# The second feed-forward product of a two-layer encoder, by seven products of halves instead of eight

## The reference

```python
D_MODEL = 1024
SEQ = 512
DEPTH = 2
D_FF = 4 * D_MODEL
...
        h = layer_norm(DN_ALPHA * h + mix @ w_out[l], ln1_g[l], ln1_b[l])
        ffn = jnp.square(jax.nn.relu(h @ w1[l])) @ w2[l]
        h = layer_norm(DN_ALPHA * h + ffn, ln2_g[l], ln2_b[l])
```

## Time and profile before

| what | value |
|---|---|
| median of 3 runs | 1117.92 us (1117.54 to 1117.95) |
| the profiled execution, its own time | 1117.77 us |
| its span in the profile | 1116.1 us |
| TensorE busy | 1098.9 us (98%) |
| VectorE busy | 606.4 us (54%) |
| ScalarE busy | 391.5 us (35%) |
| GpSimd busy | 92.0 us (8%) |
| mean granted TensorE clock | 0.999 |

### The profile page before, as it was taken

How to read it: one execution, slowest core, us unless ns; L and a number is a source line. 1 busy time by engine, 2 the same in 40 slices (tenths; PEclk the granted TensorE clock), 3 DMA queues, 4 the chain that set the end, 5 groups by cost and what they waited for, 6 DMA issues and landing times.

```text
span 1116.1 us, 15149 instructions
## 1 busy us (share of the span) xinstructions
PE 1098.9 (98%) x5502; PEld 931.2 (83%) x5502; DVE 606.4 (54%) x908; ACT 391.5 (35%) x634; POOL 92.0 (8%) x84
## 2 busy tenths in 40 slices
PE   7999999999999999999999999999999999999997
PEld 6888889988888888888878888889888888888886
DVE  7846887853443334336657478787532542433446
ACT  3433665351232232142124256553411511421410
POOL 5200222100000000000102013221000000000001
PEclk9999999999999999999999999999999999999999
DMA  7432032142223113114203410313322223123202
GB/s 276 151 114 76 1 95 77 41 156 77 98 76 128 75 75 150 75 76 151 76 7 147 151 38 21 113 39 122 113 110 79 78 96 127 75 75 139 79 10 75
DMA packets 16800, 104.38 MB, mean 94 GB/s; under 512 B 1952, under 2 KB 2384, under 8 KB 5216
## 3 DMA queue, kind: packets, MB, share of 16 engines
q1 hardware_dynamic: 15408, 97.59, 23.6%
q0 software_dynamic: 1184, 5.86, 1.6%
q10 hardware_dynamic: 144, 0.07, 0.0%
HBM read 100.37 MB, written 2.10 MB: 92 GB/s over the span
## 4 chain that ended last, share of the span: by engine, by line
PE 94%; DVE 4%; issue 1%; DMA 1%; ACT 0%; DVEq 0%; SPq 0%
PE bank L366 28%; PE bank L367 28%; PE bank L368 28%; PE bank L616 3%; PE bank L602 2%; PE bank L513 1%; PE bank L514 1%; PE bank L375 1%; DMA x<-in_x 1%; DVE x L1033 1%; PE bank L526 1%; PE bank L447 1%; DVE mx L1257 0%; DVE h_lo L1054 0%; DVE bn L1015 0%
## 5 line engine op out<-in xcount | busy, mean ns | idle before, releaser
L366 PE MATMUL bank<-h_hi,w_hi 128*128 128x512 f32 (+1 forms) x704 | 260.8, 370 | 0.1
L367 PE MATMUL bank<-h_lo,w_hi 128*128 128x512 f32 (+1 forms) x704 | 260.3, 370 | 0.0
L368 PE MATMUL bank<-h_hi,w_lo 128*128 128x512 f32 (+1 forms) x704 | 260.3, 370 | 0.0
L366 PE MATMUL bank<-w_hi,hid_hi 128*128 128x512 f32 x512 | 199.3, 389 | 0.0
L367 PE MATMUL bank<-w_lo,hid_hi 128*128 128x512 f32 x512 | 199.2, 389 | 0.0
L368 PE MATMUL bank<-w_hi,hid_lo 128*128 128x512 f32 x512 | 199.2, 389 | 0.0
L756 ACT CAST w_hi<-w_raw 128x2048 fp32r<-128x2048 f32 x60 | 112.3, 1908 | 245.1 <-PE bank L368 220.3
L366 PEld LDWEIGHTS bank<-h_hi,w_hi 128*128 128x128 f32 x704 | 132.7, 188 | 23.4 <-issue 0.9
L1367 DVE TENSOR_TENSOR x<-bank,x 128x512 f32<-128x512 f32 x64 | 44.2, 690 | 198.2 <-PE bank L368 197.9
L368 PEld LDWEIGHTS bank<-h_hi,w_lo 128*128 128x128 f32 x704 | 132.7, 188 | 22.5
L367 PEld LDWEIGHTS bank<-h_lo,w_hi 128*128 128x128 f32 x704 | 132.7, 188 | 22.2
(11 more groups left out here) (152 smaller groups left out, 1312.0 us busy)
## 6 DMA issues: line engine op xcount, KB each, us to landing
w_raw<-in_weights SPq DMA_DIRECT2D x86, 1024.0 KB, 4.8
rows<-in_rows POOLq DMA_DIRECT2D x4, 1024.0 KB, 4.9
w_raw<-in_weights SPq DMA_DIRECT2D x4, 512.0 KB, 7.5
out_h<-x SPq DMA_DIRECT2D x8, 256.0 KB, 2.0
x<-in_x SPq DMA_DIRECT2D x3, 512.0 KB, 9.6
qk_gain<-in_qk_gain POOLq DMA_DIRECT2D x3, 192.0 KB, 3.3
x<-in_x SPq DMA_DIRECT2D x2, 256.0 KB, 3.5
dft<-in_dft SPq DMA_DIRECT2D x1, 512.0 KB, 10.2
```

The source lines that it names most:

```text
L366: pe.matmul(dst, s_hi, m_hi, start=first, stop=False)
L367: pe.matmul(dst, s_hi, m_lo, start=False, stop=False)
L368: return pe.matmul(dst, s_lo, m_hi, start=False, stop=last)
```

## The change

The second stage of each chunk is computed from four quarters of the hidden matrix (A, tokens by hidden channels) and four of the weights (B, hidden channels by output channels). Halves of tokens are 256, halves of hidden channels 512 (the even and the odd tiles of the chunk), halves of output channels 512. With S1 = A21 + A22, S2 = S1 - A11, S3 = A11 - A21, S4 = A12 - S2 and T1 = B12 - B11, T2 = B22 - T1, T3 = B22 - B12, T4 = B21 - T2 the seven products are, in this order, A11 B11, S1 T1, S2 T2, S4 B22, S3 T3, A12 B21, A22 T4. Each has 2 tiles of 128 tokens, 4 steps and `three`: 24 matmuls of 128x512. A11 B11, S2 T2, S3 T3 and A22 T4 go on in the same two banks (6 and 7), S1 T1 and S4 B22 in banks 4 and 5, A12 B21 in its own two (2 and 3). After each product VectorE adds the banks as they stand to the stream: 14 additions a chunk.

What goes with it:

- ScalarE writes the relu to `y`, squares it there, and copies high parts of 256, 512 and 1024 columns; VectorE no longer squares. It makes the four sums (`hid_sum`, 256 columns each) for each of the 4 pairs of hidden tiles, and low parts of 256, 512 and 1024 columns.
- Eleven operands instead of eight blocks go through the split of each chunk. The four differences T1 to T4 are VectorE subtractions of 128x2048, written over a raw place.
- There is a third raw place, `w_third`, for B22, B21 and the next chunk's first block. To make room, working buffers of the attention part lie over the hidden ones, and `rope`, `dft`, `head_dft` and `dist` are loaded again for the second layer.
- The SP queue is written out. At the layer change it loads those four tensors and then the next weight blocks.
- GpSimd waits for the last hidden low part of the layer before it loads the normalisation rows, which lie in the same memory as `hid_sum`.
- The first four hidden tiles of chunks 2 to 4 no longer share their steps; all eight go one after the other.
- In the last chunk tiles 0 and 1 of the stream are finished by A12 B21, tiles 2 and 3 by A22 T4.

The core of the diff, constants first:

```diff
-CHUNK_G = 16
+HALF_TOK = SEQ // 2
+HALF_KT = KT // 2
+CHUNK_G = 22
+CHUNK_OPERANDS = 11
+W0, W1, W2, W3, B11, T1, T2, B22, T3, B21, T4 = range(CHUNK_OPERANDS)
+SLOT = (0, 1, 2, 3, 0, 1, 2, 3, 0, 1, 2)
+RELEASED = {W2: 0, W3: 0, B11: 2, T1: 4, T2: 6, B22: 8, T3: 10, B21: 12, T4: 14}
+NEXT_RELEASED = (18, 20)
...
```

The SP queue, per layer:

```diff
+                with sp.If(l > 0):
+                    wait(sp, l, "w_lo", 1)
+                    sp.dma_start(rope[:], rope_in).then_inc(const_landed, 16)
+                    sp.dma_start(dft[:], dft_in).then_inc(const_landed, 16)
+                    sp.dma_start(head_dft[:], head_dft_in).then_inc(const_landed, 16)
+                    sp.wait_ge(sems["products"], l * PER_LAYER["products"])
+                    sp.dma_start(dist[:], dist_in).then_inc(const_landed, 16)
...
+                    split_up_to(W0)
+                    if c == 0:
+                        load(b + 2, 0)
+                    else:
+                        load_third(b + 6)
+                    split_up_to(W1)
+                    load(b + 3, 1)
+                    split_up_to(W2)
+                    load(b + 4, 0)
+                    split_up_to(W3)
+                    load(b + 5, 1)
...
+                    split_up_to(B22)
+                    load_third(b + 7)
...
```

TensorE:

```diff
+                def half_product(a, b, dst, t, kt, first):
+                    q = slice(t * P, (t + 1) * P)
+                    s_hi, s_lo = hid_hi[:, kt, a, q], hid_lo[:, kt, a, q]
+                    m_hi, m_lo = w_cols(SLOT[b], kt, BANK, 0, BANK)
+                    start, stop, goes_on = first and kt == 0, kt == HALF_KT - 1, not first
+                    pe.matmul(bank[dst + t][:], s_hi, m_hi, start=start, stop=False, skip_group_check=goes_on)
+                    pe.matmul(bank[dst + t][:], s_hi, m_lo, start=False, stop=False, skip_group_check=goes_on)
+                    done = pe.matmul(bank[dst + t][:], s_lo, m_hi, start=False, stop=stop, skip_group_check=goes_on)
...
+                    for a, b, dst, first, n in ((S2, T2, 6, False, 1), (S4, B22, 4, False, 3), (S3, T3, 6, False, 5),
+                                                (A12, B21, 2, True, None), (A22, T4, 6, False, 9)):
+                        operand_ready(c, b)
+                        for t in range(2):
+                            if n is not None:
+                                added(n + t)
+                            for kt in range(HALF_KT):
+                                if last_chunk and b == T4 and (t, kt) == (0, 3):
+                                    with pe.If(l < DEPTH - 1):
+                                        turn(l + 1, 0)
+                                half_product(a, b, dst, t, kt, first)
...
```

VectorE in the second stage and at the end of a layer:

```diff
+                    other_quarters(3)
+                    add(0)
+                    low(T2)
+                    sum_weights(l, c, T3)
+                    add(1)
+                    low(B22)
+                    add(2)
+                    add(3)
+                    low(T3)
+                    add(4)
+                    add(5)
+                    sum_weights(l, c, T4)
+                    low(B21)
+                    add(6)
+                    add(7)
+                    low(T4)
+                    add(8)
+                    add(9)
+                    if not last:
+                        low(CHUNK_OPERANDS + W0)
+                        add(10)
+                        add(11)
+                        low(CHUNK_OPERANDS + W1)
+                        add(12)
+                        add(13)
+                        return
+                    k = 2 * l + 2
+                    add(10)
+                    variance(k, 0, 5)
+                    normalise(k, 0)
+                    add(11)
+                    variance(k, 1, 6)
+                    centre(k, 1)
+                    with dve.If(l < DEPTH - 1):
+                        stream_low(l + 1, 0, 0)
+                    scale(k, 1)
+                    with dve.If(l < DEPTH - 1):
+                        for part in range(PARTS):
+                            split_part(l + 1, 0, part)
+                        stream_low(l + 1, 0, 1)
+                    add(12)
+                    variance(k, 2, 7)
+                    normalise(k, 2)
+                    with dve.If(l < DEPTH - 1):
+                        for part in range(PARTS):
+                            split_part(l + 1, 1, part)
+                    add(13)
+                    variance(k, 3, 8)
+                    with dve.If(l < DEPTH - 1):
+                        stream_low(l + 1, 0, 2)
+                    normalise(k, 3)
```

More of the change, by code:

```diff
@@ L314, in turned_quad, with operand, raw_of @@
             return src, (slice(None), slice(2 * g, 2 * g + 2), slice(t * P, (t + 1) * P))
-        def chunk_bank(g, last):
-            return bank[(g + 4) % 8 if last else g]
+        def operand(l, c, i):
+            return l * PER_LAYER["w_lo"] + c * CHUNK_OPERANDS + (MLP0 + i)
+        def raw_of(i):
+            if i in (B22, B21, CHUNK_OPERANDS + W0):
+                return w_third[:]
+            return w_raw[:, 1 if i in (W1, W3, T3, CHUNK_OPERANDS + W1) else 0, :]
         block = ctx.enter_context(nc.Block())
@@ L646, in _, with hidden @@
                 side(last_sides[3])
[L649 to L650 removed]
+                def hidden(m, kt, t0, t1, first, last):
+                    s_hi, s_lo = w_cols(m // 2, kt, 2 * P, (m % 2) * P, P)
                     c = slice(t0 * P, t1 * P)
                     return three(bank[m][:, c], s_hi, s_lo, h_hi[:, kt, c], h_lo[:, kt, c], first, last)
[L654 to L669, removed]
[L670 to L678 removed]
@@ new lines, in add @@
+                    def add(n):
+                        p, t = n // 2, n % 2
+                        ready, dst, half, tile, before = ((1, 6, 0, 0, None), (3, 4, 1, 2, None), (5, 6, 1, 0, None), (7, 4, 1, 0, 4),
+                                                          (9, 6, 1, 2, 2), (11, 2, 0, 0, 0), (13, 6, 0, 2, None))[p]
+                        dve.wait_ge(sems["products"], l * PER_LAYER["products"] + c * CHUNK_G + (MLP_G0 + 8 + ready + t))
+                        dve.wait_ge(sems["added"], l * PER_LAYER["added"] + c * CHUNK_ADDS + (32 if before is None else 32 + before + t + 1))
+                        xs = x[:, tile + t, half * BANK:(half + 1) * BANK]
+                        dve.tensor_tensor(xs, bank[dst + t][:], xs, ALU.add).then_inc(sems["added"], 1)
+                        if last and p in (3, 4, 5, 6):
+                            wait(dve, l, "added", 32 + CHUNK_ADDS * (CHUNKS - 1) + n + 1)
+                            row_stats(tile + t, half)
@@ L1484, in _ @@
                 load_params(l + 1)
+                wait(pool, l, "hidden_lo", 12 * CHUNKS)
                 load_rows(2 * l + 2)
```

366 lines of the change are left out of this document (227 added, 139 removed).

## The result

| | before | after |
|---|---|---|
| median of 4 runs, us | 1117.93 (1117.54 to 1118.04) | 1082.52 (1081.60 to 1083.23) |
| ratio, 95% interval | | 0.9683 (0.9672 to 0.9695) |
| profiled execution, its span, us | 1117.77, 1116.1 | 1081.96, 1080.2 |

One further execution of the changed kernel (1329.5 us) and one of the kernel before (1379.9 us) ran at a mean granted clock of 0.75 and are left out; all other times are from executions at 0.98 or more.

What follows compares the result with a forecast made beforehand. TensorE, busy for 98% of the span, was taken as the bound. Chunks -43.5, end +5.3 and layer change +1.8 sum to -36.4 us from 1117.77, so 1081.4 by that clock, stated as 1081.5 us; range 1078.5 to 1091.

Steps and rivals of the forecast that it cites:

- eight chunks: Second stage: 168 matmuls for 192 saves 5.44 us in each of 8 chunks, -43.5 us; a chunk takes 81.6 us.
- the end: Behind the last matmul: VectorE finishes four tiles at E+9.9 in place of 4.6 us, +5.3 us.
- layer change: Between layers: VectorE's tiles, `h_lo` pairs and quarter splits delay tile 2's product, +1.8 us.
- no gain at all: Rival: matmuls going on in a bank already read cost 0.65 us more at 56 starts; about 1118 us, 2%.
- The added work: Per chunk beside TensorE: VectorE 60.0 us of 81.6, ScalarE 39 us, all hidden if operands are ready in time.
- The spares: Second stage of a chunk: no product waits for operands; smallest spare 2.5 us, so added work costs nothing.
- Late operands: Rival: spares of 2.5 to 4.5 us in the chunks are used up; 1084 to 1092 us, 14%.
- the walk: Step-by-step timing of a second stage from the last hidden tile's end T; chunk ends T+38.1, smallest spare 2.5 us.
- Four tiles at 4.51 from there: At the end: VectorE starts at tile 0's product, 8.16 us before TensorE's end E, and ends at E+9.9.
- The clock at the layer change: Rival: TensorE's pauses there drop the clock to 1.2 GHz, 16 matmuls cost 3.6 us more; 1085 us, 2%.
- VectorE as the bound: Rival: two-input VectorE work in the chunks is stretched past 81.6 us; at 1.5, 1149 us; 4%.
- point of break-even: Whole change lost when a chunk costs 4.5 us more than 81.6, at a VectorE stretch of 1.44.

Runs made afterwards that it cites:

- experiment 3: Changed kernel with B22's low part made twice in each chunk, 2.2 us more VectorE work; 1087.30 us.
- experiment 10: Changed kernel with B21's load issued when T3's low part is made, 3.6 us later, in every chunk; 1089.30 us.
- experiment 4: Changed kernel with B22's low part made three times in each chunk; 1113.3 us.
- experiment 1: Changed kernel with the difference T3 made ahead of the last hidden tile in every chunk; 1082.34 us, ratio 0.9682.
- experiment 2: Changed kernel without three of four contraction steps of S3 T3, 18 matmuls fewer per chunk, result incomplete; 1058.58 us.
- experiment 6: Changed kernel with A12 B21 ahead of S3 T3 in each layer's last chunk, so tiles 0 and 1 finish earlier; 1084.89 us.
- experiment 7: Changed kernel with A12 B21 ahead of S3 T3 in last chunks and the difference T3 made ahead of the last hidden tile; 1080.64 us.
- experiment 5: The changed kernel run again unedited; 1081.89, 1082.08, 1082.16, 1082.53 and 1083.30 us, the profiled run being the one of 1083.30.

## Why the prediction was right, point by point

The span fell by 35.9 us. The terms, as forecast and as measured in the profiles:

| term | forecast | measured | from |
|---|---|---|---|
| eight chunks | -43.5 | -43.5 | from tile 2's start to the last matmul 512.03 us for 533.80, twice |
| the end | +5.3 | +5.7 | 10.3 us for 4.6 behind the last matmul |
| layer change | +1.8 | +1.4 | 15.34 us for 13.94 |
| start of the program | 0 | +0.5 | first product at 12.22 us for 11.69 |
| sum | -36.4 | -35.9 | |

- **The matmuls.** Right. The seven products cost what 168 matmuls cost. Banks that are taken up again after a read cost nothing: no idle time before 448 matmuls of L750, and chunks of 81.6 us. The rival "no gain at all" is out. It had counted 56 such starts; there are 8 in a chunk, 64 in all, so its price was 0.57 us each and not 0.65.
- **The added work.** 60.0 us of VectorE forecast, 57.2 busy; 39 of ScalarE, 38.6. The difference of 2.8 us is overlap: I had added up durations, and consecutive operations of VectorE overlap by 0.08 us or so. The unknown price of 1024 columns was taken as 1.22 us and was 1.226.
- **The spares.** Right in that every product finds its operands ready: experiments 3 and 10 show that 2.3 us of VectorE and 3.4 us of loading are hidden. "Late operands" did not come. But the walk left out one place: bank 4, taken up again by S4 B22, has a spare of 2.4 us, a little less than the 2.5 at bank 7 that it called the smallest. Experiment 4 ran into it (a wait of 2.1 for 4.6 more). The 2.5 at bank 7 is untested.
- **The end.** Right in size, with the wrong reason. The step "Four tiles at 4.51 from there" starts at tile 0's product. The start is set twice over: by tile 0's product, and by VectorE's unbroken work from the last hidden tile on, which happen to meet within 0.2 us. That the forecast came out is luck in this term. Experiment 1 shows the first (VectorE waits 1.1 us for tile 0's product once it has less to do). Experiments 2 and 3 show the second: with less TensorE work VectorE's last stretch kept its 46.9 us, with one more subtraction it grew by as much. Experiments 6 and 7 show that both have to move.
- **The clock at the layer change.** This rival had 2% and 3.6 us. In experiment 5's profile it came, for 1.6 us at the layer change. Of the changed kernel's nine executions six lie at 1081.6 to 1082.5 us, with a mean granted clock of 0.995 or 0.996, and three at 1083.1 to 1083.3, with 0.993 or 0.994; this fits the same fall, though one profile alone of this kernel shows it. The weak place is the row taken as evidence: 0.80 of 2.00 us busy at clock 1.00 was one stretch and no rule. The prediction also took the Trainium skill, TensorE: Matmul & The Clock Gate, section "HAM oscillation — how this bites in real kernels", further than it goes: the waits described there are longer than these pieces, so by it this rival's time did not follow. The fall would also explain why the first four runs have a median 1 us above the forecast while the profiled execution lies 0.5 above.
- **The start.** Not in the sum. The first transposes, eight that took 1.04 us before, took 1.92; in experiment 6 they took 1.52 and the first product started at 11.70, so this 0.5 us varies from run to run.
- **VectorE as the bound** did not come in the chunks, but it holds for the last chunk of each layer. The forecast's point of break-even, all of VectorE's work stretched by 1.44, was much too generous: experiment 4 added 4.6 us to 57 in one place and lost 31 of the 35 us. Work runs into the spare behind it long before its sum reaches the chunk, and a wait of 2.1 us cost TensorE almost as much again in clock in seven chunks of eight.

## What to carry to other kernels

Where an engine works without a pause up to the end, ask how much it has to do from there on, not only when its inputs are ready; a reordering pays only with work taken off that stretch, and the two have to be tried together. Hidden work is free up to its smallest spare, so a walk through one period in order, with the queue's order and the loads in it, gives the time better than busy shares do. For each place that an engine takes up again, list every addition and low part that it waits for: the spare that the walk left out was the one that was hit. In this kernel a wait of 2.1 us in the middle of matmuls cost twice its length in seven cases of eight, while one of 1.6 us (experiment 3) cost no clock.

## What was not expected of the hardware

A pause of TensorE of 2.10 us was enough to halve its clock for 3.0 to 3.5 us of full work, in seven cases; an eighth, of 2.17 us, was not, nor one of 1.61 us at experiment 3's layer change. The 2.70 us of experiment 10 and the 3.42 us of experiment 2, at the layer change too, were. At the changed kernel's layer change pieces of at most 0.9 us, 1.1 to 1.2 us of the 4 from 548 to 552 us, did it in one profile and not in another, at nearly the same times.
